# Keeping the router keys in a row taken from the expert ring, and routing the first half tile in three steps

## What is computed

```
q = (xb @ q_w).reshape(PEER_BLOCK, PEER_HEADS, 2, PEER_DQ // 2)      # 8 heads, 2 halves of 128
s = einsum('thcd,hcnd->thcn', q, sub_keys)                          # 128 keys per head and half
s1, i1 = top_k(s[:, :, 0], 16);  s2, i2 = top_k(s[:, :, 1], 16)
cand = s1[..., :, None] + s2[..., None, :]                          # 256 candidates
cidx = i1[..., :, None] * 128 + i2[..., None, :]
top_s, pos = top_k(cand, 16);  eidx = take_along_axis(cidx, pos)
g = softmax(top_s);  u = expert_u[eidx];  v = expert_v[eidx]
a = gelu(einsum('td,thkd->thk', xb, u))
y = einsum('thk,thkd->td', g * a, v)
```

## Time and profile before

| | us |
|---|---|
| median of 3 runs (lowest, highest) | 1937.91 (1937.32, 1948.46) |
| the profiled execution, its own time | 1946.51 |
| its span in the profile | 1944.6 |
| busy: PE, DVE, ACT, POOL | 1490.2, 1258.6, 763.5, 783.3 |

### The profile page before, as it was taken

How to read it: one execution, slowest core, us unless ns; L and a number is a source line. 1 busy time by engine, 2 the same in 40 slices (tenths; PEclk the granted TensorE clock), 3 DMA queues, 4 the chain that set the end, 5 groups by cost and what they waited for, 6 DMA issues and landing times.

```text
span 1944.6 us, 27857 instructions
## 1 busy us (share of the span) xinstructions
PE 1490.2 (77%) x9567; PEld 832.6 (43%) x9567; DVE 1258.6 (65%) x3411; ACT 763.5 (39%) x2179; POOL 783.3 (40%) x676
## 2 busy tenths in 40 slices
PE   7868777969689988869668879689789785866535
PEld 4747643436345533446214447345455242423101
DVE  1565777945878788845986655984565645443755
ACT  1431345742355567642246642232222323232322
POOL 0000234423234354522443334776565767422532
PEclk9989887888789998978868989889899777786858
DMA  9986999989999999999999999999999999999997
GB/s 395 335 318 233 420 408 419 421 337 415 415 387 405 410 420 403 375 421 420 419 421 398 420 420 419 390 390 401 360 379 387 360 398 348 402 410 392 382 414 301
DMA packets 133447, 756.73 MB, mean 389 GB/s; under 512 B 17182, under 2 KB 36542, under 8 KB 47282
## 3 DMA queue, kind: packets, MB, share of 16 engines
q0 software_dynamic: 82432, 578.86, 73.7%
q1 hardware_dynamic: 50875, 176.10, 23.4%
HBM read 750.19 MB, written 9.29 MB: 391 GB/s over the span
## 4 chain that ended last, share of the span: by engine, by line
PE 29%; DVE 19%; DMA 18%; issue 7%; ACT 6%; POOL 5%; another core or an unknown queue 1%; SPq 0%; ACTq 0%; DVEq 0%
PE bank L1463 11%; DMA expert_rows<-in_expert_uv,expert_index 10%; DVE expert_rows L2768 8%; PE bank L1206 3%; POOL weight_units L2816 3%; PE bank L860 3%; PE bank L1334 3%; POOL expert_rows L2812 2%; PE bank L1190 2%; PE bank L797 2%; DMA weight_units<-in_w_out_units 2%; DMA weight_units<-in_peer_q_units 1%; DMA gate_or_shift_and_scale<-mod_dram 1%; DVE gate_or_shift_and_scale L2226 1%
## 5 line engine op out<-in xcount | busy, mean ns | idle before, releaser
L2812 POOL DMA_INDIRECT expert_rows<-in_expert_uv,expert_index x544 | 641.4, 1179 | 1095.2 <-PE bank L1463 747.7
L2768 DVE CUSTOM_DVE_ANT_0 expert_rows<-expert_rows,h_rows 128x1024 f32<-128x1024 f32 x544 | 660.6, 1222 | 300.3 <-DMA expert_rows<-in_expert_uv,expert_index 280.9
L1463 PE MATMUL bank<-expert_rows,weight_diagonals 64*64 64x512 f32 x4096 | 605.0, 708 | 143.0 <-ACT weight_diagonals L2048 130.0
L2028 ACT ACTIVATE group_gelu<-group_dots 128x2 f32<-128x2 f32 x272 | 55.8, 205 | 757.8 <-DVE group_dots L2768 677.2
L1463 PEld LDWEIGHTS bank<-expert_rows,weight_diagonals 64*64 64x64 f32 x4096 | 153.9, 151 | 430.5 <-issue 237.9
L2048 ACT ACTIVATE weight_diagonals<-consts_sb,group_weights 128x64 f32<-128x64 f32 (+1 forms) x544 | 159.0, 340 | 16.7 <-ACT group_weights L2038 0.7
L1206 PE MATMUL bank<-stage_room,weight_units 128*128 128x128 f32 x1024 | 129.2, 286 | 13.9 <-ACT stage_room L1867 7.4
L1206 PEld LDWEIGHTS bank<-stage_room,weight_units 128*128 128x128 f32 x1024 | 122.7, 199 | 34.9 <-issue 22.1
L2038 ACT ACTIVATE group_weights<-group_gelu,expert_gate 128x1 f32<-128x1 f32 x544 | 131.6, 289 | 9.4
L2028 ACT ACT_TABLE_LOAD x74 | 94.9, 1283 | 1.3
L2226 DVE SCALAR_TENSOR_TENSOR conv_out<-stage_room,small_weights,conv_out 128x128 f32<-128x128 f32 (+1 forms) x360 | 94.9, 310 | 0.1
(11 more groups left out here) (392 smaller groups left out, 1983.1 us busy)
## 6 DMA issues: line engine op xcount, KB each, us to landing
weight_units<-in_peer_q_units SPq DMA_DIRECT2D x40, 1024.0 KB
weight_units<-in_w_in_units SPq DMA_DIRECT2D x23, 1024.0 KB
weight_units<-in_w_out_units SPq DMA_DIRECT2D x19, 1024.0 KB
weight_units<-in_w_ada_units SPq DMA_DIRECT2D x13, 1024.0 KB
expert_rows<-in_expert_uv,expert_index POOLq DMA_INDIRECT x544
weight_units<-in_w_units SPq DMA_DIRECT2D x8, 1024.0 KB
expert_rows<-in_w_ada_units SPq DMA_DIRECT2D x7, 1024.0 KB, 11.0
gate_or_shift_and_scale<-mod_dram SPq DMA_DIRECT2D x11, 512.0 KB
```

Source lines behind the costliest of these rows:

```text
L1463: last = mm(e.bank[2 * a + c][o * HD:(o + 1) * HD, :], e.diag[ps, m % (NG * GR)], e.ring[ps, m % RING, cs], start=first, stop=final)
L2028: do(e.act_v[:, p], e.dots[:, p], ACT.Gelu_apprx_tanh).then_inc(e.s_gelu, 1)
L2768: vec.tensor_tensor_reduce(out=row, in0=row, in1=e.h2[:, i % 2], scale=1.0, scalar=0.0, op0=ALU.mult, op1=ALU.add, accum_out=e.dots[:, q % ...
L2812: pool.indirect_dma_start(e.ring[:, n % RING], None, e.io["expert_uv"], bass.IndirectOffsetOnAxis(ap=e.eidx[:, i % 2, j:j + 1], axis=0)).t ...
```

## The change

The keys get a home of their own and are loaded once. The array expert_rows keeps its size of ten buffers, but only nine are used for rows (`RING` = 9); the tenth holds both halves of the keys from tile 0 on. It held, before the rows began, tile 0's h (turned) and its shift, so the two loads wait for the same events as before (s_x1 and s_h2). The eight key units of tiles 1 to 4 go out of the order of the units.

Tile 0's first four heads are routed in three steps: head 0, head 1, heads 2 and 3. POOL waits for one semaphore before row 0 and another before row 16. The exponent is one instruction for four heads, 18 slots into ACT's lane, and the gates of all four heads are made behind the third step. For all other tiles the instructions of the routing and their order stay as they were.

```diff
@@ -51,7 +51,7 @@
 PE_AT = 9
 UNIT = 2048
 SLOTS = 3
-RING = 10
+RING = 9
 GR = 2
 NG = 4
 LEAD = 4
@@ -324,7 +324,8 @@
     e.consts = e.sb("consts_sb", [P, C_W])
     e.ident = e.consts[:, C_ID:C_ID + P]
     e.small = e.sb("small_weights", [P, max(b for _, b in SMALL.values())])
-    e.ring = e.sb("expert_rows", [P, RING, 2 * D])
+    e.ring = e.sb("expert_rows", [P, RING + 1, 2 * D])
+    e.keys = [e.ring[:, RING, half * D:(half + 1) * D] for half in range(2)]
     e.unit = e.sb("weight_units", [P, SLOTS, UNIT])
     e.room = e.sb("stage_room", [P, 5440])
     x_even = e.sb("x_rows", [P, D])
@@ -617,9 +618,8 @@
         "z": lambda i: [("in", i, u) for u in range(5)],
         "cmp": lambda i: [("w1", i, kv, one) for kv in range(2) for one in range(2)],
         "mix": lambda i: [("wo", i, q) for q in range(4)],
-        "query0": lambda i: [("pq", i, u) for u in range(4)] + ([("keys", i, 0)] if 0 < i < PT else []),
-        "query1": lambda i: ([("pq", i, u) for u in range(4, 8)] + ([("keys", i, 0)] if i == PT else [])
-                             + ([("keys", i, 1)] if i else [])),
+        "query0": lambda i: [("pq", i, u) for u in range(4)],
+        "query1": lambda i: [("pq", i, u) for u in range(4, 8)],
         "sc": lambda part: [("pages", part // 2, part % 2 * 2 + s) for s in range(2)],
         "satt": lambda i: [(a, hi, b) for hi in range(2) for a in ("sk", "sv") for b in range(4)],
     }
@@ -1250,22 +1250,18 @@
         sum_of_sample(2 * half + 1)
         yield
 
-    def key_half(i, half):
-        if i == 0:
-            pe.wait_ge(e.s_k0[half], 16)
-            return (e.mod_a, e.mod_b)[half].rearrange("p (a n) -> p a n", a=PH)
-        return units.take(("keys", i, half))[:, 0:D].rearrange("p (a n) -> p a n", a=PH)
+    def key_half(half):
+        pe.wait_ge(e.s_k0[half], 16)
+        return e.keys[half].rearrange("p (a n) -> p a n", a=PH)
 
     def scores_of(i, half):
-        keys = key_half(i, half)
+        keys = key_half(half)
         prod.freed(pe, ("pq", i, 2 * half + 1))
         for q in range(2):
             out = prod.open(pe, ("scores", i, 2 * half + q))
             for a in range(4):
                 last = mm(out[:, a * P:(a + 1) * P], e.q2T[:, 4 * q + a, 0:P], keys[:, 4 * q + a], start=True, stop=True)
             last.then_inc(prod.ready, 1)
-            if q and i:
-                units.used_by(("scores", i, 2 * half + 1))
             yield
 
     def query0(i):
@@ -1286,7 +1282,7 @@
             for q in range(2):
                 yield from queries(i, range(2 * q, 2 * q + 2))
                 if q == 0:
-                    keys = key_half(i, 0)
+                    keys = key_half(0)
                 prod.freed(pe, ("pq", i, q))
                 out = prod.open(pe, ("scores", i, q))
                 for a in range(4):
@@ -1308,16 +1304,12 @@
             prod.freed(pe, ("pq", i, 3))
             out = prod.open(pe, ("scores", i, 0))
             for half in range(2):
-                keys = key_half(i, half)
+                keys = key_half(half)
                 for q in range(2):
                     for a in range(4):
                         last = mm(out[(2 * half + q) * NS:(2 * half + q + 1) * NS, a * P:(a + 1) * P],
                                   e.q2T_s[:, 8 * half + 4 * q + a, 0:NS], keys[:, 4 * q + a], start=True, stop=True)
-                if half:
-                    last.then_inc(prod.ready, 1)
-                    units.used_by(("scores", i, 0))
-                else:
-                    units.used(last)
+            last.then_inc(prod.ready, 1)
 
     def sc(part):
         kv, half = part // 2, part % 2
@@ -1932,12 +1924,11 @@
 
     def topk(i, part):
         if i == 0 and part == 0:
-            for a in range(2):
-                for _ in range(7 if a == 0 else 10):
-                    yield
-                act.wait_ge(e.s_sx if a else e.s_sx0, 1)
-                g = e.gsm[:, 0, 2 * a * TK:2 * (a + 1) * TK]
-                do(g, g, ACT.Exp).then_inc(e.s_gx if a else e.s_gx0, 1)
+            for _ in range(18):
+                yield
+            act.wait_ge(e.s_sx, 1)
+            g = e.gsm[:, 0, 0:4 * TK]
+            do(g, g, ACT.Exp).then_inc(e.s_gx, 1)
             return
         n = 4 if i < PT else 2
         for _ in range(21 if i < PT else 11):
@@ -2027,11 +2018,7 @@
         act.wait_ge(e.s_dot, GR * (q + 1))
         do(e.act_v[:, p], e.dots[:, p], ACT.Gelu_apprx_tanh).then_inc(e.s_gelu, 1)
         o = GR * q - FIRST[i]
-        if GR * q == 0:
-            act.wait_ge(e.s_gt0, 1)
-        elif GR * q == 2 * TK:
-            act.wait_ge(e.s_gt, 1)
-        elif o % 64 == 0:
+        if o % 64 == 0:
             act.wait_ge(e.s_gt, 2 * i + o // 64 + 1)
         act.wait_ge(e.s_gelu, q + 1)
         for j in range(GR):
@@ -2526,17 +2513,24 @@
 
     def topk(i, part):
         if i == 0 and part == 0:
-            first = routed(0, 0, 2, 0, (e.s_sx0, e.s_gx0, e.s_gt0, e.s_rt0))
-            second = routed(0, 0, 2, 2, (e.s_sx, e.s_gx, e.s_gt, e.s_rt))
-            for n, _ in enumerate(itertools.chain(first, second)):
-                if n % 2:
+            steps = [routed(0, 0, 1, 0, e.s_rt0[0]), routed(0, 0, 1, 1, e.s_rt0[1]), routed(0, 0, 2, 2, e.s_rt)]
+            for n, _ in enumerate(itertools.chain(*steps, gates_of(0, 0, 4))):
+                if n % 3 == 2:
                     yield
         elif i < PT or part == 0:
-            yield from routed(i, part, 4 if i < PT else 2, 0, (e.s_sx, e.s_gx, e.s_gt, e.s_rt))
-
-    def routed(i, part, nh, head, sems):
-
-        shifted, exponent, gates_ready, indices_ready = sems
+            yield from routed(i, part, 4 if i < PT else 2, 0, e.s_rt)
+            yield from gates_of(i, part, 4 if i < PT else 2)
+
+    def gates_of(i, part, nh):
+        gs = e.gsm[:, i % 2, 64 * part:64 * part + nh * TK].rearrange("p (h k) -> p h k", h=nh)
+        dve.wait_ge(e.s_gx, 2 * i + part + 1)
+        link(vec.tensor_reduce(e.gsum[:, 0:nh], gs, AX, ALU.add))
+        link(vec.reciprocal(e.gsum[:, 0:nh], e.gsum[:, 0:nh]))
+        vec.tensor_tensor(gs, gs, span(e.gsum[:, 0:nh], 2, TK), ALU.mult).then_inc(e.s_gt, 1)
+        yield
+
+    def routed(i, part, nh, head, indices_ready):
+
         keep = e.top16[part]
         scores = e.scores[part][:, 2 * head:2 * (head + nh)]
         cand = scores.rearrange("p (h c) n -> p h (c n)", c=2)
@@ -2568,16 +2562,18 @@
             link(last)
             yield
 
-        for a in range(nh // 2):
+        for a in range((nh + 1) // 2):
             prod.freed(dve, ("scores", i, 2 * part + head // 2 + a))
-            yield from top16(scores, keep.half, keep.half_i, range(4 * a, 4 * a + 4))
+            yield from top16(scores, keep.half, keep.half_i, range(4 * a, min(4 * a + 4, 2 * nh)))
         pair = keep.half[:, 0:2 * nh].rearrange("p (h c) k -> p h c k", c=2)
         link(vec.tensor_tensor(grid, span(pair[:, :, 0], 3, TK), span(pair[:, :, 1], 2, TK), ALU.add))
         yield
-        for a in range(nh // 2):
-            yield from top16(cand, keep.top, keep.top_i, range(2 * a, 2 * a + 2))
+        for a in range((nh + 1) // 2):
+            yield from top16(cand, keep.top, keep.top_i, range(2 * a, min(2 * a + 2, nh)))
         top, top_i = keep.top[:, 0:nh], keep.top_i[:, 0:nh]
-        vec.tensor_tensor(gs, top, span(top[:, :, 0], 2, TK), ALU.subtract).then_inc(shifted, 1)
+        last = vec.tensor_tensor(gs, top, span(top[:, :, 0], 2, TK), ALU.subtract)
+        if not (i == 0 and part == 0 and head < 2):
+            last.then_inc(e.s_sx, 1)
         vec.tensor_copy(keep.half_f[:, 0:2 * nh], keep.half_i[:, 0:2 * nh])
         vec.tensor_single_scalar(keep.place[:, 0, 0:nh], top_i, 4, ALU.logical_shift_right)
         link(vec.tensor_single_scalar(keep.place[:, 1, 0:nh], top_i, 15, ALU.bitwise_and))
@@ -2597,10 +2593,6 @@
         vec.tensor_copy(e.eidx[:, i % 2, at:at + nh * TK].rearrange("p (h k) -> p h k", h=nh),
                         keep.picked[:, 0, 0:nh]).then_inc(indices_ready, 1)
         yield
-        dve.wait_ge(exponent, 1 if head == 0 and nh == 2 and i == 0 else 2 * i + part + 1)
-        link(vec.tensor_reduce(e.gsum[:, 0:nh], gs, AX, ALU.add))
-        link(vec.reciprocal(e.gsum[:, 0:nh], e.gsum[:, 0:nh]))
-        vec.tensor_tensor(gs, gs, span(e.gsum[:, 0:nh], 2, TK), ALU.mult).then_inc(gates_ready, 1)
 
     def sc(part):
         kv, half = part // 2, part % 2
@@ -2801,8 +2793,8 @@
     for i in range(TILES):
         for j in range(heads(i) * TK):
             n = FIRST[i] + j
-            if n == 0:
-                pool.wait_ge(e.s_rt0, 1)
+            if n in (0, TK):
+                pool.wait_ge(e.s_rt0[n // TK], 1)
             elif n == 2 * TK:
                 pool.wait_ge(e.s_rt, 1)
             elif j % 64 == 0:
...
@@ -2961,10 +2951,10 @@
                          ).then_inc(e.s_pt, 16)
         if key == ("pq", 0, 2):
             sp.wait_ge(e.s_x1, 1)
```

(4 more changed lines are left out.)

9 lines of the change are left out of this document (2 added, 7 removed).

## The result

The changed kernel takes 1963.1 us in the median of four runs (1958.0 to 1977.0) beside 1937.6 us for the kernel before; the ratio is 1.0101, with a 95% interval from 1.0058 to 1.0144. That is slower by 11 to 28 us. (The ratios in this document are those on record; they are not the quotients of the medians, which here is 1.0132, 25.5 us.) The forecast was 1941, its range ended at 1962: the change is on the edge of "within 1%", the median just outside the range, and 1937.6 times the ratio, 1957, inside it.

The account below looks back on a forecast made before the run. Compute-bound and DMA-bound stretches were taken to alternate, the DMA near full at 420 GB/s. Keys -9.5, ring +12.5, pages +2, units -4, start 0 gave +1, called +3: 1941 against 1937.91; own range 1930 to 1952, eight in ten 1924 to 1962.

Parts of the forecast that it names:

- The ring at the passages: Where compute-bound stretches turn DMA-bound, one row less is in hand: 2.5 us at five stalls, +12.5 us, bounds 0 and 30.
- the twelve stalls: Separate places between 205 and 1930 us with DMA share under 0.90, missing about 21 us; each predicted wider by up to 2.5.
- The sample pages: In the sample tile's attention, page fetches queue on POOL behind waiting rows: +2 us, bounds 0 and 10.
- The tail: PE takes four rows at once there; nine buffers leave two queued: no cost, bounds 0 and 1 us per six groups.
- The keys' bytes: Eight key loads, 4.19 MB at 420 GB/s, leave the DMA: 9 to 10 us less, entered as -9.5 us.
- the -4 us for less company of units: Where PE waits for a unit, fewer rows share the DMA queue: 4 us gained, range 0 to 12.
- The start: First row fetch 7.0 us earlier, near 184, but the ring fills and the hole moves: 0 us, bounds 7 gain, 3 loss.
- The exponent: ACT's single exponent stands behind its copy, which may go about 2 us sooner; PE's next product comes at 210: no effect.
- the ring's depth binds: Slower rival: each of 12 stalls costs 2.5 us, 30 less the keys' 10: 1958, or 1968 with pages; chance 0.24.
- a chain share of 15%: Sign: row landings' share of the chain stays near 10%; a rise to 15% would speak for the slower rival.
- the window count: Sign: 5-us windows with DMA share under 0.90, at most 20; 40 or more would mean the slower rival holds.
- The faster rival: The tenth row was spare and keys and start both pay in full: 1921, or 1915 with units' relief; chance 0.13.

Follow-up runs that it names:

- e1: The kernel before with nine row buffers alone (RING = 9; key loads and two-step routing kept): 1973.0 us, ratio 1.0129.
- e9: Nine rows alone on the kernel before, run once more as a partner for later runs: 1973.0 us, ratio 1.0121.
- e8: The kernel before, ten buffers, but the 224 odd rows away from the twelve stalls wait as in a ring of nine: 1953.3 us, ratio 1.0057.
- e10: The kernel before with nine rows and no key loads (PE reads the bias array instead, two-step routing kept): 1970.7 us, ratio 1.0131.
- e12: The kernel before with nine rows, keys still loaded but the bias array read in their place, so other experts are picked: 1971.1 us, ratio 1.0131.
- e2: The kernel before with ten rows and without the eight key loads (PE reads the bias array instead): 1947.9 us, ratio 1.0019.
- e4: The changed kernel run again, unchanged: 1964.6 us, ratio 1.0100 to the kernel before.
- e6: The changed kernel with the old two-step routing and its two exponents put back: 1959.3 us, ratio 1.0079 to the kernel before.
- e7: The kernel before, ten buffers, but 44 odd rows near the twelve stalls wait as in a ring of nine: 1955.1 us, ratio 1.0055.
- e5: The kernel before with eight row buffers alone (RING = 8): 2020.3 us, ratio 1.0402.
- e3: The kernel before with the three-step routing and single exponent alone, ten rows and key loads kept: 1944.6 us, ratio 0.9983.

## Why the prediction failed where it did, point by point

**The ring at the passages: the right mechanism, the wrong size.** The prediction took 12.5 us, five passages of 2.5 us, and 2 for the sample pages; nine rows alone cost 25 us. Its inputs, one by one:
- The price of a row, 2.5 us. The one late row that can be followed alone, row 33, costs 2.2 to 3.4 us, so the price was about right. The step of 6.0 us in e1 from row 32 to 40 has more in it than this row.
- The delay of an odd row. The average of 6.3 us hides what matters: at row 33 it is 14.2 us, the length of PE's pause.
- The count, which was the failing input. "Five of them only" was read from landings in the chain. With nine rows the starts of the dot products show 14 steps up of over 2 us in e1 and 12 in e9 (and four and three down), and about half of the loss lies away from the twelve stalls (e8), where the prediction had put "nothing".
- The clock, which the sum did not hold. A part of the 25 us goes with a lower granted clock (last section); whether nine rows cause it is open.

**The sample pages: 2 us, with a bound of 10.** Rows 432 to 480 take 3.7 to 7.5 us more in the four profiles e1, e9, e10 and e12 (from +20.7 to +28.0 in e1). It is inside the bound. But page fetches run from 1212.9 to 1668.0 in the kernel before, over passages too, and no run parts the two. **The tail: nothing.** About right: from row 480 to 543 the loss stays in e1 (+28.0 to +28.2), e9 adds 2.5 and e12 takes 1.3 off.

**The keys' bytes: -9.5 us.** This step failed in its reasoning. A share of 1.00 over 50 us was taken to mean that bytes taken away shorten the stretch. With ten rows their absence gave 1.0019, where 9.5 us would be 0.995. With nine it gave 1.0131 against a control of 1.0131. The reading that fits is that SP and POOL issue as early as buffers allow, so that the DMA is full without the stretch waiting for its end, and most of the bytes turned into idle share. No run shows the -4 us for less company of units either: e2, which has both, came out at no gain. Only the three runs where the keys stay in the tenth row (1.0101, 1.0100, 1.0079) lie some 3 per mille under the four other ratios of nine rows (1.0129, 1.0121, 1.0131, 1.0131). Whether this is a small gain of that form or chance is open. The profiles lean to a gain: at row 543 the four nine-row profiles without key loads (after, e4, e6, e10) are at +11.5 to +20.7 us, the three with them (e1, e9, e12) at +26.9 to +33.1, and the gap of their means grows from 3.6 to 7.6 us between rows 80 and 128, behind tile 1's loads. The medians of e9, e10 and e12 do not bear it out.

**The sentence from the Trainium skill on the fixed 2 us of each transfer** (SBUF — State Buffer, The DMA setup-cost knee) would have made the keys worth 26 us, as an estimate. The runs bear that out even less than the bytes: eight loads fewer gave 1.0019. **The sentence from the Trainium skill on too few buffers** (Perfetto Trace Analysis, Optimization Strategy) is the one that the runs agree with: 28 windows under 0.90 where there were 15, and 43 with eight rows. It does not reach the half of the loss that came with hardly more idle DMA (e8).

**The start.** Head 0's indices come 9.5 us behind its first MAX8 (175.21 to 184.71), for 8.6 predicted; the first fetch at 185.65, for 184.1: MAX8 itself started 0.6 us later and the routing took 0.9 longer. The tenth fetch still waits for PE, 30.63 us, and a hole stands at 220 to 230, as said. The gain goes at the first passage: the kernel after is at -3.4 us at row 32 and -0.1 at row 40, its second profile at -9.1 and -1.8. These 3 to 9 us are not the routing's either: e7, e8 and e5, with the old routing, are ahead by 4.1 to 6.4 us at row 0 too, and e3 with the new one is at +0.2. What differs is visible on PE: up to row 0 e7 is the same program as the kernel before, but the last products of the queries run through in one and come in pieces in the other. The kernel before, then e7:

```profile
204.09 0.37 PE L1206 MATMUL bank<-stage_room,weight_units 128*128 128x128 f32 x1 [0.35 <-issue]
205.50 5.20 PE L1206 MATMUL bank<-stage_room,weight_units 128*128 128x128 f32 x28 [1.04 <-issue]
```

```profile
201.55 3.84 PE L1208 MATMUL bank<-stage_room,weight_units 128*128 128x128 f32 x32 [0.57 <-DMA weight_units<-in_peer_q_units]
```

What breaks them up is open. Zero for the start was right.

**The exponent.** Wrong in the order: the prediction put ACT's copy ahead of the single exponent. The copy stands behind the exponent, at 204.56 after 204.40, where the old ones ran at 201.09 and 200.96; PE's scores wait 5.04 us and start only at 205.23. The prediction called this free because what follows needs PE's next product at 210; here PE's products ended at 200.20, so the copy was late. And DVE goes from the gates (210.03) straight into the next MAX8 (210.17): the 6.48 us of cover in the earlier trace rows are gone, because ACT's scores were ready sooner here. The third step then has no cover. The runs with and without it (1.0100 and 1.0079; 0.9983 on ten rows) can't tell 2 us.

**The rivals.** The slower one, "the ring's depth binds", named 30 us for the ring less 10 for the keys, 1958 to 1968, and 1963.1 is in it. It had a chance of 0.24, and the better half of the argument: its ring term is nearly what was measured; it is its -10 that did not come, so its range was met by two errors that offset each other in part. The sign that I set for it, a chain share of 15%, came to 14%; the window count, 28, lies between the marks of 20 and 40. The faster rival (1921) took both fillers of the DMA at their full worth; apart, on ten rows, neither showed any (1.0019 and 0.9983).

## What to carry to other kernels

A busy share of 1.0 on a prefetching DMA can mean that issuers run ahead, and not that bytes bound the stretch: before bytes are counted as time, ask what waits for the last of them. A buffer of a prefetch ring was worth more the fewer there were (25 us, then 54), and about half of the first one's worth lay away from the idle stretches of the DMA. To price a buffer, I would count the consumer's pauses longer than the mean release interval as well (6.3 us here, against 14.2 at row 33); that this count gives the right sum no run here shows.

## What the runs showed that was not expected

The time of an execution goes with its mean granted clock. Of the 11 runs of the kernel before beside e12, the two shortest (1931.58 and 1931.62 us) had 0.859, the longest (1958.75) 0.832. Over all 68 runs of that kernel beside the experiments, 0.01 less goes with some 9 us more (my estimate, a straight line through them, session by session). The nine-row runs have a lower clock than the kernel before beside them: 0.846 against 0.854 (e1), 0.846 against 0.855 (e9), 0.846 against 0.848 (e12), in the mean of the runs. By that line 2 to 8 of their 25 to 27 us go with the clock, and some 17 to 25 us are left for the row at a like clock. Whether the clock falls because PE stands more with nine rows, or the two only came together, no run tells.

One wait comes and goes between executions of the same program. In the first profile of the kernel after, DVE stands 9.75 us for a run of small stores of the sample tile's values to land; in the kernel before the same instruction (line 2443 there) does not wait:

```profile
758.34 0.56 DVE L2430 CUSTOM_DVE_ANT_0 stage_room<-bank,prompt_bias 128x384 f32<-128x384 f32 x1 [9.75 <-DMA out_new_win_sample<-sample_values]
```

```profile
751.25 0.56 DVE L2443 CUSTOM_DVE_ANT_0 stage_room<-bank,prompt_bias 128x384 f32<-128x384 f32 x1
```

In the chain of the first profile after, SP's last issue of these stores ends near 735 and the landing takes 23.25 us; in e6 it is 23.38 us with a wait of 10.3, in e3 19.45 with 5.0, in e8 15.30 with 1.1, and the second profile after has no wait at all. It comes with either ring depth and with either routing, and the two profiles of one program differ in it, so it is not the change's; it can be a part of the scatter of 20 us between runs of one kernel. What sets the landing is open.
